# A new order for the attention stretch of a two-block kernel: queries ahead of the convolution's mean, norms behind later work, splits in steps of two tiles

## The chip, the cores and the metric

One core of one Trainium2 chip runs the whole program. The time is the device time of one execution in microseconds (us); the median of three runs counts. A core has five engines with a queue of instructions each: PE (TensorE, matrix products), DVE (VectorE), ACT (ScalarE), POOL (GpSimd) and SP (SyncE, which issues most of the loads). Each works through its queue in program order and waits on counters (semaphores) that other engines raise.

## What is computed

The reference is a chain of two transformer-like blocks on 256 tokens of width 2048, in float32. The change touches the middle of the first block only: the convolution branch, attention, and the beginning of the product with `w_out`.

```python
h = rmsnorm(x, pre_mix_norm)
conv_in, q_lat, kv_lat, k_rope = split(h @ w_in)
a, g = split(conv_in)                       # 1024 channels each
u = causal_depthwise_conv(a * sigmoid(g), conv_w, conv_b)   # 31 taps
u = silu(layernorm(u, conv_ln_g, conv_ln_b))
q = rmsnorm(q_lat, q_norm) @ w_uq           # 8 heads, 128 plain + 64 rotary columns
k_nope, v = rmsnorm(kv_lat, kv_norm) @ w_ukv
attn = causal_attention(q, k, v)            # softmax, 8 heads
mix = concat(rmsnorm(u, conv_out_norm), rmsnorm(attn, attn_out_norm)) @ w_out
x = x + rmsnorm(mix, post_mix_norm)
x = x + rmsnorm(swiglu(rmsnorm(x)), post_ffn_norm)
# second block: pooling mixer, RG-LRU, then 8 heads x 16 experts per token,
# whose rows are gathered from two tables by index
```

## The kernel before

Activations lie transposed in SBUF: a tile is 128 channels by 256 tokens, so 1024 channels are 8 tiles. Weights come through a ring of four 1 MB slots (`raw`); SP issues the load of a unit when the unit four places earlier is no longer used. There are two kinds of units. Plain ones (`w_ukv`, `w_uq`) are used by PE as they are. Those of the wide products (`w_in`, `w_out`, the feed-forward) are split: ACT rounds a piece to a high part (`weights_hi`, into `whi`), DVE subtracts it to get the low part (`weights_lo`, into `wlo`), and the input is split in the same way into `xhi` and `xlo`. A unit is two pieces of 128 output columns over 8 input tiles; for each piece PE issues 8 matmuls of `whi` with 512 columns (both input parts) and 8 of `wlo` with 256 columns (`half_group`). Pieces of `w_out` come in this order: the first half of the input (tiles 0 to 7, the convolution's) for four pieces, then the second half (tiles 8 to 15, attention's) for the same columns. After these eight pieces a loop (`layer`) does the rest.

Nothing schedules the work: the order on each engine is the order in which its block of the program is written, and a wait holds up all that stands behind it in that queue. The names on which the steps below rest:

- `add_taps` (DVE, L1804): the 31 taps of the depthwise convolution, 2 x 31 instructions for each pair of channel tiles, put between other work since the input projection; the remainder runs behind the key rotation.
- the mean (PE, L946): 8 products of a matrix of ones with `conv_a`, waiting for all taps. Its result goes to bank 2; DVE centres the 8 tiles (L1849).
- `head_queries(n, half)` (PE, L922): the queries of head pair n, in two halves of the depth, each from one unit of `w_uq`. ACT copies them out (`queries_out`, L1226). `rotate` (PE, L932) and `rope` (DVE, L1853 to L1857) rotate the 64 rotary columns.
- `pair(n, between)`: `scores` of both heads (PE, L966 and L968), then what `between` holds, then the transposes of the probabilities (L981) and the products with the values (L988, L989). For a head DVE masks and finds the maximum (`head_scores`, L1870 to L1877), ACT takes the exponentials (L1373, L1375), DVE divides (`normalise`, L1884 to L1886), ACT copies the transposes and the outputs.
- A norm goes through three engines: ACT squares the tiles (`norm_squares`, L1238), PE sums them with ones (`norm_total`, L766), DVE takes mean and reciprocal (`norm_inverse`, L1717 and L1720), ACT the root (`norm_root`, L1245), DVE multiplies the tiles (`finish` or `norm_finish`, L1892, L1730). Three norms stand here: `ln` (the layer norm on the centred convolution), `conv` (after Silu, L1395, on ACT) and `attn`.
- `SPLITS` gives at which count of split steps each product's input starts. The input of `w_out` was split in four steps of four tiles.

```python
            pair(0, between_0)
            pair(1, between_1)
            pair(2, lambda: head_queries(3, 1))
            pair(3, lambda: half_group(PIECE0["out1"], 0, PAIRS[0], arriving="out1"))

            half_group(PIECE0["out1"] + 2, 0, PAIRS[1])
            norm_total(NI["attn"], tmp)
            half_group(PIECE0["out1"] + 4, 1, PAIRS[0], arriving="out1")
```

## Time and profile before

| | |
|---|---|
| median of 3 runs | 2808.8 us (2808.61 to 2814.53) |
| the profiled execution | 2809.3 us |
| its span in the profile | 2807.4 us |
| busy PE, DVE, ACT, POOL | 85%, 62%, 28%, 19% of the span |
| mean granted PE clock | 0.975 of full speed |
| the stretch of the change | from 214.3 us (last keys and values) to 347.6 us (loop of `w_out`) |

The profile is one execution. Start times are microseconds from the start of the span. A row of the timeline merges like instructions of one engine: its start, its length, and in brackets the idle time before it with what ended it. PE shows two rows for a float32 product of 128x256, so the 8 products of a total stand as x16. The ends of matmuls are modelled and overlap the next start by some 0.15 us; the time that a block of them takes is therefore read from start to start. A table load (ACT_TABLE_LOAD) is what ACT does when it changes between exponential, Silu and square root. The granted clock is 1.00 at 2.4 GHz and 0.50 at 1.2 GHz.

### The profile page before, as it was taken

The page shows a single profiled execution, that of the slowest core. Times are in us where ns is not written, and L with a number is a line of the kernel's source. Part 1 is how long each engine was busy: PE and PEld are TensorE (multiplying, and loading weights), DVE is VectorE, ACT ScalarE, POOL GpSimd, SP SyncE. Part 2 cuts the span into 40 slices and gives each one's busy share as a digit, 9 for nine tenths or more (in the row PEclk, how much of TensorE's full clock was granted, in tenths as well). Part 3 has the DMA queues.
Part 4 walks back from the last instruction along what each step waited for, and adds up shares of the span by engine and source line. Part 5 has one row for each costly group of instructions (what it writes and reads, how often), then busy time and mean ns, then how long its engine had stood idle before and what let it go on. Part 6 is the DMA issues. An engine that isn't in the chain of part 4 may idle for free.

```text
span 2807.4 us, 29432 instructions
## 1 busy us (share of the span) xinstructions
PE 2379.4 (85%) x10942; PEld 1695.0 (60%) x10942; DVE 1745.5 (62%) x2556; ACT 789.6 (28%) x1156; POOL 520.4 (19%) x594
## 2 busy tenths in 40 slices
PE   8997799999999999899899757777777777777776
PEld 8996688888888888799788622222222232222222
DVE  6985547665666566587657985555655555555444
ACT  5433454443444344545431101001100110111010
POOL 0000010000000000100012343333333333333341
PEclk9999899999999999999999989999999999999999
DMA  6542354556555655554588999999999999999997
GB/s 218 177 129 74 93 177 151 193 181 193 184 190 181 193 180 167 161 165 151 167 256 318 416 421 422 422 422 421 421 422 421 421 421 422 421 421 421 422 422 323
DMA packets 339901, 798.92 MB, mean 285 GB/s; under 512 B 23313, under 2 KB 270699, under 8 KB 273771
## 3 DMA queue, kind: packets, MB, share of 16 engines
q0 software_dynamic: 73728, 536.90, 46.0%
q1 hardware_dynamic: 262971, 257.82, 29.0%
q10 hardware_dynamic: 3120, 3.15, 0.3%
q8 instruction: 47, 0.77, 0.1%
q14 instruction: 35, 0.29, 0.0%
HBM read 795.72 MB, written 2.10 MB: 284 GB/s over the span
## 4 chain that ended last, share of the span: by engine, by line
DMA 38%; PE 12%; DVE 7%; issue 1%; POOL 1%; ACT 1%; DVEq 0%; POOLq 0%; PEldq 0%
DMA row<-in_peer_v,expert 31%; DMA row<-in_peer_u,expert 7%; PE pl L808 4%; DVE row L2269 3%; PE pl L1199 3%; PE pl L815 3%; PE pl L811 1%; PE pl L812 1%; POOL row L719 1%; DVE wlo L1745 1%; DMA raw<-in_w_out 0%; PE pl L1128 0%; DVE x_split L1967 0%; DVE tmp L1958 0%; DVE l_xc L2155 0%
## 5 line engine op out<-in xcount | busy, mean ns | idle before, releaser
L1199 PE MATMUL pl<-row,diag 128*128 128x512 f32 x1856 | 862.1, 608 | 337.7 <-DMA row<-in_peer_v,expert 333.3
L2269 DVE CUSTOM_DVE_ANT_0 row<-row,pg 128x2048 f32<-128x2048 f32 x256 | 582.1, 2287 | 458.0 <-DMA row<-in_peer_u,expert 456.7
L1199 PEld LDWEIGHTS pl<-row,diag 128*128 128x128 f32 x1856 | 338.6, 192 | 861.2 <-issue 467.2
L1745 DVE TENSOR_TENSOR wlo<-raw,whi 128x1024 fp32r<-128x1024 f32 (+1 forms) x436 | 517.3, 1208 | 388.1 <-ACT whi L1226 386.5
L1226 ACT ACTIVATE whi<-raw 128x1024 fp32r<-128x1024 f32 (+1 forms) x436 | 444.1, 1039 | 417.0 <-PE pl L815 400.1
L808 PE MATMUL pl<-x_split,whi 128*128 128x512 f32 x1888 | 479.2, 396 | 23.3 <-DVE x_split L1753 12.0
L808 PEld LDWEIGHTS pl<-x_split,whi 128*128 128x128 f32 x1888 | 342.9, 191 | 87.6 <-issue 13.5
L815 PE MATMUL pl<-x_split,wlo 128*128 128x256 f32 x2656 | 373.5, 284 | 3.8 <-DVE wlo L1745 3.8
L815 PEld LDWEIGHTS pl<-x_split,wlo 128*128 128x128 f32 x2656 | 359.1, 192 | 23.0 <-DVE wlo L1745 4.2
L719 POOL DMA_INDIRECT row<-in_peer_u,expert x256 | 240.9, 941 | 635.5 <-PE pl L1199 504.6
L1647 ACT ACTIVATE diag<-ident,dots 128x128 f32<-128x128 f32 x232 | 90.8, 400 | 889.0 <-PE pl L1199 861.0
L719 POOL DMA_INDIRECT row<-in_peer_v,expert x256 | 252.0, 984 | 168.5 <-issue 65.5
L687 POOL TENSOR_TENSOR sq_sum<-mix 128x512 f32<-128x512 f32 x2 | 2.6, 1292 | 1071.8 <-ACT mix L1508 725.1
L811 PE MATMUL pl<-x_split,whi 128*128 128x256 f32 x768 | 190.2, 285 | 4.6 <-DVE x_split L1753 2.5
L812 PE MATMUL pl<-x_split,whi 128*128 128x256 f32 x768 | 189.1, 284 | 0.0
L808 PE MATMUL pl<-h_split,whi 128*128 128x512 f32 x704 | 179.1, 395 | 4.3 <-DVE h_split L2013 2.2
L811 PEld LDWEIGHTS pl<-x_split,whi 128*128 128x128 f32 x768 | 147.9, 193 | 6.4 <-issue 5.7
L812 PEld LDWEIGHTS pl<-x_split,whi 128*128 128x128 f32 x768 | 148.0, 193 | 0.1
L808 PEld LDWEIGHTS pl<-h_split,whi 128*128 128x128 f32 x704 | 126.7, 190 | 27.1 <-issue 2.6
L1128 PE MATMUL pl<-mix,wq 128*128 128x256 f32 (+1 forms) x576 | 114.0, 360 | 2.3 <-issue 2.3
L1128 PEld LDWEIGHTS pl<-mix,wq 128*128 128x128 f32 x576 | 100.8, 194 | 13.8 <-issue 2.4
L815 PEld LDWEIGHTS pl<-h_split,wlo 128*128 128x128 f32 x704 | 97.7, 191 | 7.7
(331 smaller groups left out, 1528.8 us busy)
## 6 DMA issues: line engine op xcount, KB each, us to landing
raw<-in_w_in SPq DMA_DIRECT2D x50, 1024.0 KB, 5.4
raw<-in_w_gate SPq DMA_DIRECT2D x44, 1024.0 KB, 5.1
raw<-in_w_up SPq DMA_DIRECT2D x44, 1024.0 KB, 5.1
raw<-in_w_out SPq DMA_DIRECT2D x32, 1024.0 KB, 5.4
raw<-in_w_down SPq DMA_DIRECT2D x32, 1024.0 KB, 5.3
wq<-in_peer_wq SPq DMA_DIRECT2D x13, 1024.0 KB, 10.8
raw<-in_w_down SPq DMA_DIRECT2D x16, 768.0 KB, 4.7
raw<-in_w_ukv SPq DMA_DIRECT2D x4, 1024.0 KB, 5.1
```

Source lines behind the costliest of these rows:

```text
L687: nc.gpsimd.tensor_tensor(sq_sum[:], a, b, ALU.add).then_inc(sq_added, 1)
L719: nc.gpsimd.indirect_dma_start(row[b][:], None, A["peer_u_2" if table == "u" else "peer_v_2"][0], bass.IndirectOffsetOnAxis(ap=expert[:, a ...
L808: mm(banks[f], w, xs[:, x].rearrange("p h s -> p (h s)"), start=first_product, stop=(half == 1 and t == k - 1), skip_group_check=True)
L811: mm(banks[f][:, 0:S], w, xs[:, x, 0, :], start=first_product, stop=False, skip_group_check=True)
L812: mm(banks[f][:, 0:S], w, xs[:, x, 1, :], start=False, stop=False, skip_group_check=True)
L815: last = mm(banks[f][:, 0:S], wlo[:, n % 4, t, :], xs[:, half * k + t, 0, :], start=False, stop=(half == 1 and t == k - 1), skip_group_che ...
L1128: last = mm(bank[:, f * S + cols:f * S + cols + width], w[:, t, f, :], mix[:, half * KU + t, cols:cols + width], start=first, stop=(half = ...
L1199: last = mm(pl[q], diag[:, (at - 1) % 4, :], row[b][:, q * 512:(q + 1) * 512], start=(t == 1 and n == 0 and k == 0), stop=last_row, skip_g ...
L1226: return nc.scalar.activation(o, i, ACT.Copy)
L1647: activation(diag[:, (at - 1) % 4, :], ident[:], ACT.Copy, scale=dots[:, c:c + 1]).then_inc(diag_ready, 1)
L1745: V.tensor_tensor(wlo[:, n % 4, 0:k, :], w[:, :, f, :], whi[:, n % 4, 0:k, :].bitcast(F32), ALU.subtract)\
L2269: V.tensor_tensor_reduce(row[b][:], row[b][:], z_tok[:], 1.0, 0.0, ALU.mult, ALU.add, dots[:, at:at + 1])\
```

## The change

The same arithmetic is done, in another order.

1. **PE.** The convolution's mean moves from ahead of the first four `head_queries` and `rotate(0)` to behind them. The total of `ln` moves from ahead of the first scores into `between_0`, behind the queries of the third pair. In `between_1` the total of `conv` moves behind the queries and the rotation. The total of `attn` is cut in two: 4 tiles in `between_2`, 4 between the third and fourth piece of `w_out`.
2. **DVE.** `rope(0)` comes ahead of the centring; the inverse of `ln` comes behind `head_scores`, `normalise` and `rope(1)` of the first pair; the inverse of `conv` comes behind `normalise(3)` and `rope(2)`; the low part of the first `w_out` weights comes ahead of the inverse of `conv`.
3. **ACT.** `queries_out(1)` ahead of the squares of `ln`; `norm_root(ln)` behind the transposes of the first pair; Silu behind the outputs of the first pair; the first `weights_hi` in the second pair instead of the third; the squares of `attn` in two steps of 4 tiles, into `sq_ln` and no longer into `tmp`; the high parts of the pieces 4 to 7 right behind.
4. **Splits of the input of `w_out`** in eight steps of two tiles, on ACT (`out1_hi`), DVE (`out1_lo`) and in PE's waits (`step_of=2`). For the last 8 tiles DVE takes turns: two tiles scaled by the norm, then the low part of the two before.

```diff
-SPLITS = {"in1": 0, "out1": 4, "ffn": 8, "in2": 16, "out2": 24}
+SPLITS = {"in1": 0, "out1": 4, "ffn": 12, "in2": 20, "out2": 28}
...
-            pe.wait_ge(rot_read, 1)
-            pe.wait_ge(conv_step, CONV_K * CT)
-            for t in range(CT):
-                last = mm(pg[2][:, 0:S], ones[:], conv_a[:, t, :], start=(t == 0), stop=(t == CT - 1))
-            last.then_inc(mean_sum, 1)
...
             rotate(0)
-            norm_total(NI["ln"], sq_ln)
+            pe.wait_ge(rot_read, 1)
+            pe.wait_ge(conv_step, CONV_K * CT)
+            for t in range(CT):
+                last = mm(pg[2][:, 0:S], ones[:], conv_a[:, t, :], start=(t == 0), stop=(t == CT - 1))
+            last.then_inc(mean_sum, 1)
...
                 rotate(1)
+                norm_total(NI["ln"], sq_ln)
 
             def between_1():
-                norm_total(NI["conv"], conv_a)
                 head_queries(3, 0)
                 rotate(2)
+                norm_total(NI["conv"], conv_a)
+
+            def between_2():
+                head_queries(3, 1)
+                norm_total(NI["attn"], sq_ln, 0, 4)
+
+            def between_3():
+                half_group(PIECE0["out1"], 0, PAIRS[0], arriving="out1", step_of=2)
...
-            half_group(PIECE0["out1"] + 2, 0, PAIRS[1])
-            norm_total(NI["attn"], tmp)
-            half_group(PIECE0["out1"] + 4, 1, PAIRS[0], arriving="out1")
+            half_group(PIECE0["out1"] + 2, 0, PAIRS[1], between=lambda: norm_total(NI["attn"], sq_ln, 4))
+            half_group(PIECE0["out1"] + 4, 1, PAIRS[0], arriving="out1", step_of=2)
...
+            exponentials(2)
+            exponentials(3)
+            act.wait_ge(conv_silu, CT)
+            norm_squares(NI["conv"], mix, conv_a)
+            weights_hi(u, pc, halves=(0,))
+            prob_out(2)
+            prob_out(3)
+            outputs(2)
+            outputs(3)
+            act.wait_ge(o_ready, 4)
+            activation(sq_ln[:, 0:4, :], mix[:, 8:12, :], ACT.Square).then_inc(norm_sq, 1)
+            norm_root(NI["conv"])
...
+            norm_scale(NI["attn"], HEADS * VH)
+            for t in range(8, DT + 2, 2):
+                if t < DT:
+                    for f in (t, t + 1):
+                        V.scalar_tensor_tensor(mix[:, f, :], mix[:, f, :], col("attn_out_norm", f - 8), rstd[:], ALU.mult, ALU.mult)\
+                            .then_inc(norm_out, 1)
+                if t > 8:
+                    out1_lo(t - 2)
```

PE's queue around the mean, before; `conv_a,ones` is the mean, `q_lat,raw` are the queries, `rotT` is the rotation, `sq_ln,ones` the total of `ln`, the last rows the first scores.

```order
L902 MATMUL pg<-raw,kv_lat 128x256 x8
L946 MATMUL pg<-conv_a,ones 128x256 x8
L922 MATMUL pg<-q_lat,raw 128x256 x3
L922 MATMUL pl<-q_lat,raw 128x256 x6
...
L932 MATMUL pg<-q_pe,rotT 128x256
L766 MATMUL pg<-sq_ln,ones 128x256 x8
L966 MATMUL pl<-k_nope,q_nope 128x128
L968 MATMUL pl<-k_pe,q_pe 128x128
```

And the same place after the change, with the total of `ln` ahead of the transposes of the first pair:

```order
L905 MATMUL pg<-raw,kv_lat 128x256 x8
L925 MATMUL pg<-q_lat,raw 128x256 x3
L925 MATMUL pl<-q_lat,raw 128x256 x6
...
L935 MATMUL pg<-q_pe,rotT 128x256
L956 MATMUL pg<-conv_a,ones 128x256 x8
L968 MATMUL pl<-k_nope,q_nope 128x128
...
L935 MATMUL pg<-q_pe,rotT 128x256
L766 MATMUL pg<-sq_ln,ones 128x256 x8
L983 MATMUL pg<-ident,tmp 128x128 x6
```

The eight matmuls of the mean now stand behind 36 matmuls of queries and one rotation, and the total of `ln` behind the first scores and the third pair's queries.

ACT's queue in the second head pair after the change; L1381 and L1383 are the exponentials, `conv_a<-mix` the squares of `conv`, `whi` the first pieces of `w_out`, `tmp<-pg` the transposed probabilities, `sq_ln<-mix` the first squares of `attn`, L1254 the root of `conv`.

```order
L1381 ACT_TABLE_LOAD [waits pT_done]
L1381 ACTIVATE tmp,small<-tmp,small 128x128 [waits s_max]
L1383 ACTIVATE tmp,small<-tmp,small 128x256
...
L1247 ACTIVATE conv_a<-mix 128x1024 [waits conv_silu]
L1247 ACTIVATE conv_a<-mix 128x1024
L1235 ACTIVATE whi<-raw 128x1024 [waits piece_used,slot_full3]
L1235 ACTIVATE whi<-raw 128x1024 [waits piece_used]
L1235 ACTIVATE tmp<-pg 128x384 [waits o_done,pT_done] x2
L1235 ACTIVATE mix<-pg 128x256 [waits o_done] x2
L1427 ACTIVATE sq_ln<-mix 128x1024 [waits o_ready]
L1254 ACT_TABLE_LOAD [waits norm_out]
L1254 ACTIVATE rstd<-invms 128x256 [waits norm_inv]
```

Before, the squares of `conv` stood between the two outputs of the first pair, the root of `conv` behind the exponentials of the second, and `whi` at the end of the third pair.

## Rows read from the trace of the kernel before

**Rows 1.** Stretches: start:end, us, busy PE PEld DVE ACT POOL, PEclk, DMA share, GB/s
```profile
450.00:1120.00 670.00, 664.95 (x3793) 584.35 (x3792) 409.82 (x427) 282.52 (x307) 0.00 (x0) 1.00 0.58 184
...
1800.00:2807.00 1007.00, 738.35 (x1592) 290.04 (x1592) 553.47 (x786) 105.67 (x239) 370.38 (x382) 0.99 1.00 415
```

**Rows 2.** PE in order of time, 226 to 257 us: start, us, engine, line, what
```profile
226.61 6.43 PE L946 MATMUL pg<-conv_a,ones 128*128 128x256 f32 x16 [12.34 <-DVE conv_a L1804]
...
232.88 1.46 PE L922 MATMUL pg<-q_lat,raw 128*128 128x256 f32 x6
...
248.85 3.62 PE L766 MATMUL pg<-sq_ln,ones 128*128 128x256 f32 x16
...
252.30 0.38 PE L966 MATMUL pl<-k_nope,q_nope 128*128 128x128 f32 x2
...
256.37 1.56 PE L922 MATMUL pg<-q_lat,raw 128*128 128x256 f32 x6
```

**Rows 3.** PE in order of time, from 267 us to the loop of w_out
```profile
267.56 0.55 PE L981 MATMUL pg<-ident,tmp 128*128 128x128 f32 x3 [2.17 <-DVE tmp L1886]
...
282.18 0.82 PE L981 MATMUL pg<-ident,tmp 128*128 128x128 f32 x6
...
284.66 0.39 PE L966 MATMUL pl<-k_nope,q_nope 128*128 128x128 f32 x2
...
305.30 3.75 PE L808 MATMUL pl<-x_split,whi 128*128 128x512 f32 x8 [5.68 <-DVE x_split L1753]
...
334.86 3.53 PE L808 MATMUL pl<-x_split,whi 128*128 128x512 f32 x8 [8.08 <-ACT whi L1226]
...
344.76 2.00 PE L808 MATMUL pl<-x_split,whi 128*128 128x512 f32 x8
...
347.56 2.00 PE L808 MATMUL pl<-x_split,whi 128*128 128x512 f32 x8
```

**Rows 4.** DVE (VectorE) in order of time, 233 to 335 us
```profile
233.53 2.77 DVE L1849 TENSOR_TENSOR conv_a<-conv_a,mean_b 128x256 f32<-128x256 f32 x8
...
253.03 1.75 DVE L1720 RECIPROCAL invms<-meansq 128x256 f32<-128x256 f32 x1
...
257.80 3.25 DVE L1892 SCALAR_TENSOR_TENSOR conv_a<-conv_a,par,rstd 128x256 f32<-128x256 f32 x8
...
266.64 0.16 DVE L1884 RECIPROCAL small<-small 128x2 f32<-128x2 f32 x1
...
299.21 0.55 DVE L1870 SCALAR_TENSOR_TENSOR tmp<-pl,mask 128x384 f32<-128x384 f32 x1
...
300.52 0.56 DVE L1870 SCALAR_TENSOR_TENSOR tmp<-pl,mask 128x384 f32<-128x384 f32 x1
...
332.69 2.43 DVE L1753 TENSOR_TENSOR x_split<-mix,x_split 128x1024 fp32r<-128x1024 f32 x2
```

**Rows 5.** ACT (ScalarE) in order of time, 214 to 305 us
```profile
214.80 1.08 ACT L1226 ACTIVATE v_tok<-pg 128x512 f32<-128x512 f32 x2
...
254.82 0.42 ACT L1245 ACTIVATE rstd<-invms 128x256 f32<-128x256 f32 x1 [5.61 <-DVE invms L1720]
...
255.25 1.28 ACT L1373 ACT_TABLE_LOAD   x1
...
261.08 3.30 ACT L1395 ACTIVATE mix<-conv_a,par 128x256 f32<-128x256 f32 x8 [0.87 <-DVE conv_a L1892]
...
269.93 1.99 ACT L1238 ACTIVATE conv_a<-mix 128x1024 f32<-128x1024 f32 x2
...
302.85 1.99 ACT L1226 ACTIVATE x_split<-mix 128x1024 fp32r<-128x1024 f32 x2
```

**Rows 6.** Two stretches with the granted PE clock, columns as in rows 1
```profile
252.30:299.60 47.30, 44.35 (x201) 32.60 (x199) 29.02 (x74) 26.66 (x59) 0.00 (x0) 1.00 0.29 90
...
305.30:313.41 8.11, 8.11 (x33) 6.98 (x33) 2.41 (x7) 0.00 (x0) 0.00 (x0) 0.67 0.00 0
```

**Rows 7.** DMA issues of the page: size, median us from issue to landing
```profile
raw<-in_w_out SPq DMA_DIRECT2D x32, 1024.0 KB, 5.4
```

More of the change, by code:

```diff
@@ L762, in norm_total @@
                     pe.wait_ge(norm_inv, n)
-                for t in range(tiles):
+                for t in range(t0, t1 or tiles):
                     if t % 4 == 0:
@@ L766, in norm_total @@
                     last = mm(pnorm, ones[:], sq[:, t, :], start=(t == 0), stop=(t == tiles - 1))
-                last.then_inc(norm_sum, 1)
+                if (t1 or tiles) == tiles:
+                    last.then_inc(norm_sum, 1)
             def wide_total(name):
@@ L791, in squares, with half_group @@
                     last.then_inc(norm_sum, 1)
-            def half_group(first, half, banks, xs=x_split, k=KU, i=None, step=0, arriving=None, step_of=4, apart=True):
+            def half_group(first, half, banks, xs=x_split, k=KU, i=None, step=0, arriving=None, step_of=4, apart=True, between=None):
                 for f in range(2):
                     n = first + f
+                    if f and between:
+                        between()
                     pe.wait_ge(w_hi, n + 1 if i is None else i * step + (n + 1))
@@ L1415, in _, with conv_out, out1_hi @@
-            weights_hi(UNIT0["out1"], PIECE0["out1"], halves=(1,))
+            def conv_out(tiles):
+                for c in tiles:
+                    activation(mix[:, c, :], conv_a[:, c, :], ACT.Silu, bias=col("conv_ln_b", c)).then_inc(conv_silu, 1)
+            def out1_hi(t):
+                copy(xhi[:, t:t + 2, :], mix[:, t:t + 2, :]).then_inc(x_hi, 1)
+            u, pc = UNIT0["out1"], PIECE0["out1"]
+            exponentials(0)
+            exponentials(1)
+            queries_out(2)
@@ new lines, in _ @@
+            act.wait_ge(o_ready, 4)
+            activation(sq_ln[:, 0:4, :], mix[:, 8:12, :], ACT.Square).then_inc(norm_sq, 1)
+            norm_root(NI["conv"])
+            exponentials(4)
+            exponentials(5)
+            queries_out(3)
+            prob_out(4)
+            prob_out(5)
+            outputs(4)
+            outputs(5)
+            act.wait_ge(norm_out, tiles_before(NI["conv"] + 1))
+            for t in range(0, 8, 2):
+                out1_hi(t)
+            exponentials(6)
@@ L1416, in _ @@
+            exponentials(7)
+            weights_hi(u, pc, halves=(1,))
+            prob_out(6)
+            prob_out(7)
+            outputs(6)
+            outputs(7)
             act.wait_ge(o_ready, HEADS)
-            norm_squares(NI["attn"], mix[:, 8:16, :], tmp)
+            activation(sq_ln[:, 4:8, :], mix[:, 12:16, :], ACT.Square).then_inc(norm_sq, 1)
+            weights_hi(u + 2, pc + 4, halves=(0,))
             norm_root(NI["attn"])
-            for t in range(8, DT, 4):
-                act.wait_ge(norm_out, tiles_before(NI["attn"]) + t - 4)
-                copy(xhi[:, t:t + 4, :], mix[:, t:t + 4, :]).then_inc(x_hi, 1)
+            for t in range(8, DT, 2):
+                act.wait_ge(norm_out, tiles_before(NI["attn"]) + t - 6)
+                out1_hi(t)
@@ L1424, in gains @@
+            weights_hi(u + 2, pc + 4, halves=(1,))
             def gains(a, name, norm, g, i=None):
@@ L1450, in out @@
                     gains(src, "post_mix_norm", "post", g, i)
-                weights_hi(u + 2, n + 4)
                 out(0)
@@ L1857, in rope @@
                 V.tensor_tensor(q_pe[:, n, :], q_pe[:, n, :], rot[:, n, :], ALU.add).then_inc(roped, 1)
+            add_taps(len(taps))
+            rope(0)
+            dve.wait_ge(mean_sum, 1)
+            link(V.tensor_scalar(mean_b[:], pg[2][:, 0:S], 1.0 / CONV_CH, None, ALU.mult))
+            for c in range(CT):
+                V.tensor_tensor(conv_a[:, c, :], conv_a[:, c, :], mean_b[:], ALU.subtract).then_inc(centred, 1)
             score = tmp[:, 0:4, :].rearrange("p a b -> p (a b)")
@@ L1908, in _ @@
             rope(2)
+            weights_lo(u, pc, halves=(0,))
+            norm_inverse(NI["conv"], CONV_CH)
             dve.wait_ge(conv_silu, CT)
```

74 lines of the change are left out of this document (26 added, 48 removed).

## The prediction

> **What bounds the kernel now.** I began with the busy time by stretch, to see whether time saved in attention reaches the end. In the feed-forward PE works for 665.0 of 670 us, and in the last 1007 us the DMA engines are busy all the time at 415 GB/s, with the gathered rows [rows 1]. Neither stage can make up for a late start or waste an early one: both begin when the stage before hands over, so what the attention stretch loses or wins stands in the total one for one. The question is when the loop of `w_out` starts; now it is at 347.56 [rows 3].
>
> Next, PE in order of time, from the last keys and values on. It waits 12.34 us for the convolution's taps, which keep DVE busy, and then takes the mean, in 6.3 us from start to start although the total of `ln`, equally large, takes 3.45 [rows 2]. Behind that come the queries, which need nothing of the convolution. Later PE waits 5.68 us for the splits of the convolution's tiles and 8.08 us for the weights of piece 4, which stand in ACT's queue behind the norm of attention; after both its 8 wide matmuls take 3.75 and 3.53 us instead of 2.00 [rows 3]. The granted clock tells why: 1.00 (2.4 GHz) through the head pairs, 0.67 over the two pieces behind the wait of 5.68, part of them at 1.2 GHz, so that they take 8.1 us [rows 6]. Between these, a head pair is bound by PE with one short wait (2.17 us) [rows 3].
>
> **The change, part by part.** I lay the new order out in time with the durations of the rows, hand-overs (0.05 to 0.2 us) included.
>
> *Mean behind the queries.* PE can begin when ACT has copied the last values, at 214.80 + 1.08 = 215.9 [rows 5]. Four query halves and a rotation take 248.85 - 232.88 = 16.0 us [rows 2], to 231.9. The taps end at 226.5, when the mean starts today, so they are covered with 5 us to spare; their instructions don't change. The mean at the full clock costs 3.45: 235.3. Today mean, queries and rotation are through at 248.85: 13.5 us earlier. `rope(0)` (1.2 us) falls beside the mean, and the scores can follow at once.
>
> *Total of `ln` behind the first pair's queries.* Scores take 256.37 - 252.30 = 4.1 us [rows 2], the third pair's two halves and rotation 8.2 (half of the 16.0 with one rotation kept), the total 3.45: 251.1. Transposes and values take 284.66 - 282.18 = 2.5 [rows 3]: 253.6. Cover: DVE centres in 2.8 and needs 1.3 for each head's maximum (300.52 - 299.21) [rows 4], to 241.4; ACT squares in 2.0, loads a table in 1.28 and takes two heads' exponentials in 2.0 (302.85 - 300.52 less that 1.3 is one head) [rows 4, 5], to 244.0; dividing takes 0.9 (267.56 - 266.64) [rows 3, 4], to 245.8 for both. So 5 us of slack, and the second scores start 16.6 us earlier than now (267.56 + 2.5 and hand-overs, 270.2).
>
> *The second pair: here the chain leaves PE.* From the end of the total of `ln`: mean and reciprocal 2.2 with the hand-over 0.2, root 0.42, eight tiles 3.25 [rows 4, 5], to 257.5; Silu 3.3, table 1.28, exponentials 2.0, squares 2.0 [rows 5], to 266.0. PE is through with scores, queries and rotation at 262.0 and waits about 3 us, since the total of `conv` can start on the first four squares at 265.1; it ends at 268.5. With transposes and values 271.0, against 284.66 now: 13.7 earlier. The early `weights_hi` costs ACT 1.9 us there but ends by 268, before the transposes are out; its 1 MB has had since PE's use of the third pair's first unit (243.3) and lands in 5.4 [rows 7].
>
> *The third pair.* Output copies, 1.0 of squares, the table, root, eight tiles (3.25), then on DVE two maxima (2.7), an exponential (1.0), a division (0.9), and on PE transpose, rotation, values (2.2): 284.2. Now that point is at 295.4 (305.30 less the wait of 5.68 and scores of 4.1, with the overlap of ends), so the lead is down to 11.2. PE hides the query half and the first half of the `attn` total in this chain.
>
> *Splits by two tiles, weights early.* Four hi copies of half of 1.0 us each [rows 5] and their low parts (half of 1.2 [rows 4]) run from 284.7 to 287.9; scores end at 288.3. So the wait of 5.68 goes, and with it the half clock behind it. Two pieces at 2.8 (347.56 - 344.76) [rows 3], transposes and values 2.5, piece 2, half the total (1.7): 300.9. Then the norm of attention: reciprocal 2.2, root 0.4, two tiles 0.8, hi 0.55, lo 0.65: piece 4 starts at 306.1 and its last split arrives at 309.6, as DVE needs 1.45 per step of two tiles. The rest, 1.4 + 3 x 2.8, ends at **319.5**, against 347.56.
>
> **The sum.** Laid out with the same durations, today's order gives 346.7 (with its slow clock twice, 8.1 - 5.6 = 2.5 and 3.5 - 2.0 = 1.5 us), 0.9 short of the trace; I add 0.8 to the new one: 320.3, or 27.3 us less. Against that stands the clock. The new order keeps two waits of PE, 3 us ahead of the total of `conv` and 2.5 to 3 ahead of piece 4, then 1 us between its steps. Waits of 2.17 cost nothing, those of 5.68 and more cost 1.5 to 2.8 us of slow matmuls each. Between these rows: 0 to 5.6 us; I take 3, since 3 us lies nearer to the small wait but there are two places. That leaves 24.3 us: 2809.3 of the profiled execution becomes 2785.0, and on the median of 2808.8, which is 0.5 lower, **2784.5 us**.
>
> A rule speaks against part of this. The new queue has one table load more (seven in the stretch, six now): root of `ln`, Silu, exponentials again. A row has 1.28 us for one, and the next instruction starts 0.02 behind it [rows 5]. The Trainium skill (ScalarE: Activation LUTs, "What ACT_TABLE_LOAD costs") gives about 2.66 us per switch, drain included. By its figure the sum would be 2788.6, an estimate; I go by the row.
>
> **The rivals.**
>
> *A switch of tables costs more than its row (5%).* The loads ahead of the root of `ln`, of the exponentials behind Silu and of the root of `conv` stand on my chain or at its edge. If ACT loses the row's 1.28 once more at each of three, that is 3.8 us: 2788.3. For it: nothing in the rows; the rule above is the one that says so.
>
> *The norms' chain eats more (10%).* If ACT's order costs a wait that I don't see in the second and third pairs, the lead keeps shrinking as it does from 16.6 to 11.2, and the last part wins nothing: 11.2 us, 2797.6. For it: ACT now holds weights between squares and transposes. Against it: the 8.08 and 5.68 us waits are removed by the order itself.
>
> *The mean's cover fails (3%).* If queries and taps can't run side by side (weights of the second pair not landed, say), 12.3 us of waiting stays and only the last part helps: 13 to 15 us less, 2795.
>
> *No change (3%).* Something later, a weight load for the loop of `w_out`, sets its start. Against it: SP issues by freed slots, and these come free earlier as well.
>
> *Slower: PE falls to 1.2 GHz and stays (3%).* PE now works in small groups with a wait before each: four splits per input half, squares cut in two. If the clock falls there, its work doubles. From 215.9 to 319.5 PE has some 95 us of work at the full clock; once 27 us of it run at half, the gain is gone; were it all, the time would be about 2876, and with half of it 2829. Against it: in the head pairs, with the same small groups, PE was busy 44.35 of 47.30 us and the clock stood at 1.00 [rows 6]. The Trainium skill (TensorE: Matmul & The Clock Gate, "A second HAM failure mode: psum-queue depth-cycling") says that micro-idles between groups of matmuls can make the clock oscillate; this trace doesn't show it for waits as short as these.
>
> **How the numbers follow.** My case has 76%: 2779.5 (no slow clock, a little better hand-overs) to 2791 (two slow starts at 2.8 and 4 us of hand-overs that I missed). It takes in the first rival; the others, 19%, lie outside and fill the two in ten. A measurement of this kernel can tell about 0.2%, 5.6 us. Faster by more: 94%, same 3%, slower 3%.
>
> **What would show it.** The mean (L956) starts near 232 and lasts 3.6 in one block; the second scores start near 254, the third near 271, the fourth near 284, the loop of `w_out` near 320 to 323. PE's wait ahead of the total of `conv` is about 3 us, ended by ACT's squares, and that ahead of piece 4 about 3, ended by the splits. Wrong would be: a wait of PE in the first four query halves, a wait ahead of the first scores, a table load followed by more than 0.1 us of idle ACT with its input there, or a block of slow matmuls longer than 6 us. If the loop starts near 321 and the total falls by much less, the claim on the later stages is what failed.

## The result, and the profile after

The change runs at a median of 2783.86 us (4 runs, 2781.24 to 2784.27) beside 2808.7 us for the kernel before in the same comparison (4 runs, 2807.49 to 2814.53). The ratio is 0.9906, with a 95% interval of 0.9888 to 0.9923, so 22 to 31 us less. The forecast was 2784.5. The profiled execution took 2784.27 us, its span is 25.0 us shorter than that of before.

The page of the kernel after, span and busy time:

```profile
span 2782.4 us, 29442 instructions
...
PE 2373.8 (85%) x10942; PEld 1690.4 (61%) x10942; DVE 1745.8 (63%) x2560; ACT 791.7 (28%) x1161; POOL 521.8 (19%) x594
```

The shares are what they were. Nothing was made cheaper; idle time went. So the place has to be looked for in time. PE of the kernel after, in order of time, with the points that the prediction named:

```profile
215.92 1.53 PE L925 MATMUL pg<-q_lat,raw 128*128 128x256 f32 x6 [1.71 <-issue]
...
231.97 3.62 PE L956 MATMUL pg<-conv_a,ones 128*128 128x256 f32 x16
235.42 0.38 PE L968 MATMUL pl<-k_nope,q_nope 128*128 128x128 f32 x2
...
253.73 0.39 PE L968 MATMUL pl<-k_nope,q_nope 128*128 128x128 f32 x2
...
265.26 5.38 PE L766 MATMUL pg<-conv_a,ones 128*128 128x256 f32 x16 [2.87 <-ACT conv_a L1247]
270.48 0.82 PE L983 MATMUL pg<-ident,tmp 128*128 128x128 f32 x6
...
286.77 0.46 PE L968 MATMUL pl<-k_nope,q_nope 128*128 128x128 f32 x2
...
309.14 0.70 PE L811 MATMUL pl<-x_split,whi 128*128 128x512 f32 x2 [2.56 <-DVE x_split L1929]
310.44 1.22 PE L811 MATMUL pl<-x_split,whi 128*128 128x512 f32 x2 [0.60 <-DVE x_split L1929]
311.84 2.07 PE L811 MATMUL pl<-x_split,whi 128*128 128x512 f32 x4 [0.17 <-DVE x_split L1929]
...
324.47 2.00 PE L811 MATMUL pl<-x_split,whi 128*128 128x512 f32 x8
```

The wait of 12.34 us ahead of the mean [rows 2] is gone, and so are those of 5.68 and 8.08 [rows 3]. Three are new: 1.71 ahead of the queries, which begin when ACT has copied the last values (at 215.9, as laid out), 2.87 ahead of the total of `conv`, 2.56 ahead of piece 4 with gaps of 0.60 and 0.17 behind it. The loop of `w_out`, the last row, starts at 324.47 instead of 347.56 [rows 3].

Behind two of the new waits the clock is down, as the stretches show (start:end, us, busy PE, PEld, DVE, ACT, POOL, granted clock, DMA share, GB/s). The last two rows are the feed-forward and the gathers, to be read beside [rows 1]:

```profile
265.20:270.50 5.30, 5.24 (x17) 4.31 (x18) 3.33 (x5) 2.76 (x3) 0.00 (x0) 0.68 0.29 99
309.10:316.00 6.90, 6.09 (x18) 4.38 (x19) 5.74 (x9) 3.15 (x4) 0.00 (x0) 0.57 0.01 2
...
450.00:1089.00 639.00, 636.75 (x3646) 559.99 (x3645) 388.60 (x403) 267.98 (x289) 0.00 (x0) 1.00 0.58 186
1800.00:2782.00 982.00, 720.32 (x1552) 283.01 (x1552) 538.47 (x758) 103.66 (x234) 361.71 (x372) 0.99 1.00 415
```

What fills the time ahead of the total of `conv` is ACT's queue in the second pair, after the change:

```profile
257.70 3.30 ACT L1399 ACTIVATE mix<-conv_a,par 128x256 f32<-128x256 f32 x8 [1.48 <-DVE conv_a L1925]
261.02 1.28 ACT L1381 ACT_TABLE_LOAD   x1
262.31 0.40 ACT L1381 ACTIVATE tmp<-tmp,small 128x128 f32<-128x128 f32 x1
...
264.08 1.99 ACT L1247 ACTIVATE conv_a<-mix 128x1024 f32<-128x1024 f32 x2
```

Silu ends at 261.0, and a table and two heads' exponentials go ahead of the squares that PE waits for. DVE sets the pace at piece 4, with a low part behind every two scaled tiles:

```profile
308.31 0.68 DVE L1929 TENSOR_TENSOR x_split<-mix,x_split 128x512 fp32r<-128x512 f32 x1
308.91 0.88 DVE L1972 SCALAR_TENSOR_TENSOR mix<-mix,par,rstd 128x256 f32<-128x256 f32 x2
309.70 0.69 DVE L1929 TENSOR_TENSOR x_split<-mix,x_split 128x512 fp32r<-128x512 f32 x1
...
311.09 1.48 DVE L1929 TENSOR_TENSOR x_split<-mix,x_split 128x512 fp32r<-128x512 f32 x2
```

**After the loop starts.** Up to 1092 us of the new trace the low parts of the weights on DVE, which run through all of the loops, stand 23.1 us earlier than their likes of before; then the distance jumps to 24.6. At that place PE has the same wait in both. The kernel before:

```profile
1115.22 2.10 PE L808 MATMUL pl<-h_split,whi 128*128 128x512 f32 x6 [2.03 <-ACT whi L1226]
```

The kernel after:

```profile
1092.15 1.65 PE L811 MATMUL pl<-h_split,whi 128*128 128x512 f32 x6 [2.03 <-ACT whi L1235]
```

The stretch of 5.2 us behind it, before:

```profile
1115.20:1120.40 5.20, 5.18 (x19) 4.39 (x20) 2.58 (x3) 1.48 (x2) 0.00 (x0) 0.67 0.40 101
```

And after:

```profile
1092.10:1097.30 5.20, 5.15 (x28) 4.51 (x29) 2.75 (x3) 2.16 (x3) 0.00 (x0) 1.00 0.39 107
```

Behind the same 2.03 us of idle PE the clock was at 0.67 before and at 1.00 after: 19 matmuls against 28 in equal time. That is 1.5 us that the change got at a place that its edit doesn't touch. The first gather starts 24.6 us earlier (POOL, 1487.37 and 1462.74), the last store 25.1 us (SP's queue, 2802.56 and 2777.46).

The traces of the experiments below show how far such a difference can be trusted. With the two kernels of this case they make fourteen, one trace each. In all of them the wait of 2.03 us (2.02 in some) stands 767.65 to 767.69 us behind the start of the loop, so up to there the gain is handed on whole. Behind it the clock was at 0.67 in seven traces, that of before among them, and at 1.00 in the other seven. From the loop to the end of the span they take 2455.8 to 2461.4 us, though no edit touches these stages; the kernel before has 2459.8, the change 2457.9.

### The profile page after: what moved, and what is told of

It reads as the page before. It is cut to its first block, busy times and chain, and to the rows that moved or that the text cites. A ratio compares the mean times of both kernels' runs of the same rounds, so it can differ in the third digit from the quotient of the medians.

```text
span 2782.4 us, 29442 instructions
## 1 busy us (share of the span) xinstructions
PE 2373.8 (85%) x10942; PEld 1690.4 (61%) x10942; DVE 1745.8 (63%) x2560; ACT 791.7 (28%) x1161; POOL 521.8 (19%) x594
## 4 chain that ended last, share of the span: by engine, by line
DMA 38%; PE 12%; DVE 8%; issue 1%; POOL 1%; ACT 1%; DVEq 0%; POOLq 0%; PEldq 0%
DMA row<-in_peer_v,expert 32%; DMA row<-in_peer_u,expert 6%; PE pl L811 4%; DVE row L2320 3%; PE pl L1208 3%; PE pl L818 3%; PE pl L814 1%; PE pl L815 1%; POOL row L719 1%; DVE wlo L1777 1%; DMA raw<-in_w_out 0%; PE pl L1137 0%; DVE x_split L2018 0%; DVE tmp L2009 0%; DVE l_xc L2206 0%
```

## The experiments

Totals move by 3.0 us among the four runs of the change, and by 8.5 among fourteen runs of the kernel before (2805.62 to 2814.14). So I compare the kernels by marks on PE in the profiled execution: microseconds from the start of PE's last block of values (210.65 before, 210.59 after), which no edit touches. A mark is one execution. "Change" stands for the changed kernel. The last column carries the clock with it: from piece 4 to the loop five kernels with the same steps of DVE and the same wait of 2.56 us take 15.33 (change), 13.98, 14.07, 14.77 and 15.43 us (one more table, conv splits late, squares first, chain shorter). Differences under 1.5 us at the loop can't be told from that.

| kernel | 1st scores | 2nd | 3rd | 4th | piece 0 | piece 4 | loop | time, us (runs) |
|---|---|---|---|---|---|---|---|---|
| before | 41.65 | 59.58 | 74.01 | 84.75 | 94.65 | 124.21 | 136.91 | 2808.7 (4) |
| mean alone | 35.59 | 54.82 | 69.42 | 80.16 | 90.06 | 119.94 | 132.82 | 2802.46 (10) |
| tail as before | 24.83 | 43.15 | 62.37 | 75.09 | 84.73 | 113.96 | 128.01 | 2797.7 (5) |
| conv splits late | 24.83 | 43.15 | 62.38 | 76.18 | 84.26 | 104.65 | 118.72 | 2785.98 (1) |
| weights late | 24.83 | 43.14 | 62.38 | 76.18 | 80.32 | 102.05 | 115.09 | 2782.59 (1) |
| one more table | 24.83 | 43.14 | 64.68 | 78.49 | 82.64 | 100.87 | 114.85 | 2782.47 (1) |
| splits by four | 24.83 | 43.14 | 62.38 | 76.18 | 80.33 | 100.66 | 114.72 | 2783.61 (1) |
| **change** | 24.83 | 43.14 | 62.37 | 76.18 | 80.32 | 98.55 | 113.88 | 2783.86 (4) |
| filled waits | 24.83 | 43.14 | 62.75 | 76.56 | 80.71 | 100.77 | 112.30 | 2784.32 (4) |
| filled to measure | 24.83 | 43.14 | 60.69 | 74.50 | 78.65 | 96.86 | 111.47 | 2782.67 (4) |
| squares first | 24.83 | 43.15 | 60.14 | 73.99 | 78.14 | 96.36 | 111.13 | 2779.87 (4) |
| chain shorter | 24.83 | 43.15 | 57.89 | 70.36 | 74.51 | 92.72 | 108.15 | 2778.89 (4) |
| two pieces abreast | 24.83 | 43.14 | 57.89 | 70.36 | 74.51 | 92.73 | 105.56 | 2775.0 (4) |
| the same, filled | 24.83 | 43.14 | 57.89 | 70.36 | 74.50 | 92.73 | 104.87 | 2775.14 (4) |

The kernel before ran beside each set too, with medians of 2808.6, 2808.51 and 2809.18 us.

### The mean alone

The kernel before, with only the mean moved. So that it can move, `rope(0)` goes ahead of the centring and `queries_out(1)` ahead of the squares of `ln`.

```diff
-            pe.wait_ge(conv_step, CONV_K * CT)
-            for t in range(CT):
-                last = mm(pg[2][:, 0:S], ones[:], conv_a[:, t, :], start=(t == 0), stop=(t == CT - 1))
-            last.then_inc(mean_sum, 1)
...
             rotate(0)
...
+            pe.wait_ge(conv_step, CONV_K * CT)
+            for t in range(CT):
+                last = mm(pg[2][:, 0:S], ones[:], conv_a[:, t, :], start=(t == 0), stop=(t == CT - 1))
+            last.then_inc(mean_sum, 1)
+
             norm_total(NI["ln"], sq_ln)
```

> The kernel before with only the mean moved behind the four query halves and rotate(0) (with rope(0) and queries_out(1) put ahead, which that needs). My theory: the taps' wait of 12.34 us is covered, but the total of ln now has to wait some 4.4 us for the squares of the centred tiles, since it still stands ahead of the first scores. First scores at 243 instead of 252.3, so 9 us less; with a slow PE clock behind that wait 7.5. Loop of w_out near 338.5 to 340. Rival (the mean alone is the whole gain): 13.5 us less or more, loop at 334 or earlier. Rival (cover fails, the queries wait for weights): under 3 us.

The loop came 4.1 us earlier and the time fell to 2802.46 (ratio 0.9976, 0.9966 to 0.9985), where 7.5 to 9 us had been expected. The cover held: the mean started at 231.93 with no wait. But what is behind it is now bare, in PE's time order:

```profile
231.93 3.62 PE L953 MATMUL pg<-conv_a,ones 128*128 128x256 f32 x16
240.05 6.26 PE L766 MATMUL pg<-sq_ln,ones 128*128 128x256 f32 x16 [4.50 <-ACT sq_ln L1238]
...
261.41 0.55 PE L981 MATMUL pg<-ident,tmp 128*128 128x128 f32 x3 [2.17 <-DVE tmp L1887]
```

PE waits 4.50 us for the squares and then takes 6.10 from start to start, 2.65 more than at the full clock. A second slow stretch follows at 262, behind a wait of 2.17 us that stood in the kernel before at the same place [rows 3] and cost nothing there. The two stretches of this kernel:

```profile
240.00:246.20 6.20, 6.15 (x17) 5.02 (x18) 0.00 (x0) 0.85 (x1) 0.00 (x0) 0.58 0.00 0
262.20:265.40 3.20, 3.20 (x12) 2.84 (x13) 0.00 (x0) 1.84 (x4) 0.00 (x0) 0.52 0.22 73
```

and the place of the second in the kernel before:

```profile
268.30:271.60 3.30, 3.25 (x18) 2.49 (x18) 0.00 (x0) 2.78 (x5) 0.00 (x0) 1.00 0.24 79
```

So moving the mean alone gains a third of the 12.34 us that PE waited. The first scores come 6.1 us earlier (at the full clock it would have been 8.7), the second 4.8, and 0.7 more is lost up to the loop. What stood covered behind that wait, ACT's squares of `ln`, comes to light.

### The tail as before

The changed kernel with everything from the splits on as before: steps of four tiles, first weights in the third pair, total of `attn` in one piece, weights of piece 4 last.

```diff
-                norm_total(NI["attn"], sq_ln, 0, 4)
...
-                half_group(PIECE0["out1"], 0, PAIRS[0], arriving="out1", step_of=2)
+                half_group(PIECE0["out1"], 0, PAIRS[0], arriving="out1")
...
+            norm_total(NI["attn"], tmp)
```

> The changed kernel with everything behind the third pair's scores as before: input of w_out split in four steps behind the last exponentials, weights of pieces 4 to 7 late, norm of attention in one go. My theory: the lead of 16.6 us shrinks through the norms' chain to about 12 at the last scores and nothing is won behind them, so the waits of 5.6, 1.5 and 8.1 us stand again. Loop near 336 to 338, 10 to 11.5 us less than before in all. Rival (the tail is worth nothing, its waits were hidden): loop near 325 as in the changed kernel. Rival (front is worth nothing): loop near 347.

The loop came at 128.01: of the 23.0 us of the change 8.9 are from the order of the mean, the totals and what moved with them on ACT and DVE, and 14.1 from the tail. The times say the same, 2797.7 (ratio 0.9962, 0.9948 to 0.9976), 11 and 14 us. So the totals moved along with the mean more than double what the mean gives. All marks up to the third scores are those of the change to 0.01 us, and the lead of 16.8 us at the first scores has shrunk to 9.7 at the fourth. The change's fourth scores come 1.1 us later than these (76.18 and 75.09): that is what the tail's work, put into the third pair, costs there. PE of this kernel shows the two waits of before again:

```profile
294.39 3.75 PE L811 MATMUL pl<-x_split,whi 128*128 128x512 f32 x8 [5.43 <-DVE x_split L1782]
...
323.62 3.78 PE L811 MATMUL pl<-x_split,whi 128*128 128x512 f32 x8 [8.08 <-ACT whi L1235]
```

### Three parts of the tail, each undone by itself

Splits by four tiles instead of two, with DVE scaling all tiles first:

```diff
-                copy(xhi[:, t:t + 2, :], mix[:, t:t + 2, :]).then_inc(x_hi, 1)
+                copy(xhi[:, t:t + 4, :], mix[:, t:t + 4, :]).then_inc(x_hi, 1)
...
+            norm_finish(NI["attn"], mix[:, 8:16, :], "attn_out_norm", mix[:, 8:16, :], HEADS * VH)
+            input_lo("out1", mix, (8, 12))
```

> The changed kernel with the input of w_out split in steps of four tiles instead of two, at the same places. By my layout the first x_lo of attention's tiles comes 2 us later but the last one as early, so the loop starts within 0.3 us of the changed kernel's 324.5 (plus up to 1 us if the longer wait of 4.5 us brings a longer slow clock). Rival (small steps are what wins in the tail): 3 us or more later.

The weights of pieces 4 and 5 behind the splits of attention, on ACT and DVE:

```diff
-            weights_hi(u + 2, pc + 4, halves=(0,))
             norm_root(NI["attn"])
...
-            weights_hi(u + 2, pc + 4, halves=(1,))
+            weights_hi(u + 2, pc + 4)
```

> The changed kernel with the high and low parts of pieces 4 and 5 behind attention's splits, as before. By my layout PE's wait ahead of piece 4 grows from 2.6 to 6.2 us but its steps come without gaps; loop 1.5 us later than 324.5, 2 to 3.5 with a slow clock. Rival (the wait of 8.08 was the weights' and goes with them): 5 us or more later.

The splits of the convolution's tiles behind the last exponentials and, on DVE, behind the last maxima:

```diff
+            exponentials(6)
+            exponentials(7)
             act.wait_ge(norm_out, tiles_before(NI["conv"] + 1))
             for t in range(0, 8, 2):
                 out1_hi(t)
-
-            exponentials(6)
-            exponentials(7)
```

> The changed kernel with the splits of the convolution's tiles behind the last exponentials and maxima, as before, still in steps of two tiles. My theory: here lies the largest part of what the tail wins. PE waits about 3.8 us ahead of piece 0, then 0.2 per step, and DVE comes later to everything behind: loop 4.4 us later by the layout, 6 to 7 with a slow clock, so 118 to 121 us. Rival (the steps of two tiles hide it): under 115.

The loop came 0.84, 1.21 and 4.84 us later. Each of these kernels ran once. PE at piece 4, with splits by four:

```profile
310.27 3.75 PE L811 MATMUL pl<-x_split,whi 128*128 128x512 f32 x8 [4.67 <-DVE x_split L1785]
```

and with the weights late:

```profile
311.63 3.78 PE L811 MATMUL pl<-x_split,whi 128*128 128x512 f32 x8 [6.06 <-ACT whi L1235]
```

Both open the wait by 2 to 3.5 us and yet move the loop by about 1. In the change PE starts earlier but then stops between steps; its last four matmuls begin at 311.84, 101.25 from the mark. By four tiles all eight begin at 100.66, with late weights at 102.05. What sets the end is the last split, so starting on the first is worth little.

How little, an estimate from the rows tells. At the full clock a piece takes 2.79 us. The change's last split ends at 101.98 from the mark, and 1.4 us and three pieces behind it are 111.8. With splits by four, four pieces behind 100.66 are 111.8 too, with late weights 113.2. So the small steps are worth nothing there by themselves and the early weights 1.4 us. The rest is the clock, which took 2.1 us in the change, 2.9 and 1.9 in the two others; as said above, 0.84 and 1.21 can't be told from it.

The early splits of the convolution's tiles are the part with weight. Undone, PE waits ahead of piece 0 again:

```profile
293.77 3.75 PE L811 MATMUL pl<-x_split,whi 128*128 128x512 f32 x8 [3.86 <-DVE x_split L1928]
```

Piece 0 starts 3.94 us later (84.26 for 80.32), and slow matmuls add 2.2 up to piece 4; from there to the loop the clock took 1.3 less than in the change. Together the three differences make 6.9 of the 14.1 us. The rest is in what they do jointly, in the earlier weights of the first pieces and in the total of `attn` cut in two; I did not take these apart.

### Is it the clock? Waits filled with useless matmuls

Extra work is added here: `n` matmuls of the mask by the ones, into a PSUM bank that nobody reads at that time, ahead of the total of `conv` and of piece 4. The two waits on `o_ready` keep them behind the values, whose bank they use. First 12 and 11 of them, then 6 and 5, as one takes 0.43 us (5.18 us from start to start for 12).

```diff
+                pe.wait_ge(o_ready, 2)
+                fill(12)
                 norm_total(NI["conv"], conv_a)
...
+            pe.wait_ge(o_ready, HEADS)
+            fill(11)
             half_group(PIECE0["out1"] + 4, 1, PAIRS[0], arriving="out1", step_of=2)
```

> The changed kernel with matmuls of no use in PE's two longest waits (12 ahead of the total of conv, 11 ahead of piece 4; they write a bank that nothing reads then). From the start of PE's last block of values to the loop of w_out it is 113.9 us in the changed kernel, 136.9 before. My theory: the total of conv takes 5.2 us instead of 3.45 and pieces 4 and 5 take 9.75 instead of some 7.8 only because the clock falls in these waits; filled, both go: 1.8 + 1.9 less, so 110.2 us, and 3 to 4 us in all. Rival (the total waits for its second squares, pieces 4 and 5 for their splits and weights): no change, 113.9. Rival (the clock falls by something else than the wait): partly, 112 or more.

> The changed kernel with 6 useless matmuls ahead of the total of conv and 5 ahead of piece 4, which is what fits into the waits of 2.87 and 2.56 us (one takes 0.43; the run before had 12 and 11, which pushed both points 2.2 us back and ate what the clock gave). My theory: total of conv in 3.45 us at its old start, 54.7 us behind PE's last block of values, pieces 4 and 5 without slow matmuls: 109.8 to 110.5 us to the loop instead of 113.9. Rival (only long filling holds the clock): 112 or more.

With 12 and 11, PE:

```profile
261.24 5.34 PE L1007 MATMUL pg<-mask,ones 128*128 128x256 f32 x24
266.42 3.62 PE L766 MATMUL pg<-conv_a,ones 128*128 128x256 f32 x16
...
305.81 4.91 PE L1007 MATMUL pg<-mask,ones 128*128 128x256 f32 x22
310.37 2.38 PE L811 MATMUL pl<-x_split,whi 128*128 128x512 f32 x8
```

and its clock there:

```profile
266.40:270.00 3.60, 3.60 (x19) 3.12 (x18) 2.02 (x2) 0.57 (x1) 0.00 (x0) 1.00 0.02 5
310.30:317.20 6.90, 6.90 (x38) 5.78 (x38) 3.98 (x6) 3.13 (x4) 0.00 (x0) 1.00 0.17 40
```

The filling was 2.2 us too long each time (marks 56.8 and 100.77 for 54.67 and 98.55), and still the loop starts 1.6 us earlier than in the change, because nothing behind it runs slowly. Its 112.30 is far from the 110.2 that I had expected and lies where I had put the rival of another cause, at 112 or more. But at piece 4 this kernel starts late, when all splits are there, so it doesn't part a held clock from late input.

The shorter filling does, for the first wait. With 6 and 5 the total of `conv` starts when it does in the change and the third scores come 1.7 us earlier, which is the price of that wait alone. Unfilled, the same wait (2.87 or 2.88 us) is followed by the same slow total (a row of 5.38 us) in all five kernels of the table that have this order: change, tail as before, conv splits late, weights late, splits by four. So it is PE's idling that brings the clock down there. The loop starts 2.4 us earlier, at 111.47 where 109.8 to 110.5 had been expected. The filling ahead of piece 4 did not show: from there to the loop it takes 14.61 us, within the 13.98 to 15.43 of the kernels without it. PE of that kernel at the total of `conv` and at piece 4:

```profile
264.33 3.69 PE L766 MATMUL pg<-conv_a,ones 128*128 128x256 f32 x16 [0.28 <-ACT conv_a L1256]
...
309.21 2.04 PE L811 MATMUL pl<-x_split,whi 128*128 128x512 f32 x4 [0.66 <-DVE x_split L1938]
```

The long wait was filled there, to 0.40 us, but the steps of DVE leave gaps of 0.6, and behind these the clock fell to 0.54 for 3.7 us:

```profile
309.20:312.90 3.70, 3.69 (x13) 3.18 (x14) 3.05 (x3) 1.91 (x3) 0.00 (x0) 0.54 0.00 0
```

The rule of the Trainium skill that I had set against the change (TensorE: Matmul & The Clock Gate, "A second HAM failure mode: psum-queue depth-cycling") says that micro-idles between groups of matmuls make the clock swing between its levels. This trace agrees in part: behind gaps of 0.4 to 0.66 us it fell to 0.54 once, and did not swing.

In the total the filling is not to be seen: 2784.32 and 2782.67, ratios 0.9911 and 0.9907 with the change's 0.9906. In the trace of the longer filling the stages behind the start of the loop took 2461.4 us, 3.5 more than the change's, which is more than it had won.

### One more change of tables

A square root of a 128x1 tile between Silu and the exponentials, an addition that nothing uses, makes ACT load one table more on the chain to the total of `conv`.

```diff
             conv_out(range(CT))
+            activation(small[:, 63:64], ones[:, 0:1], ACT.Sqrt)
```

> The changed kernel with one square root of 128x1 between Silu and the exponentials of the third head, which makes ACT change tables once more on the chain. By the row of 1.28 us the chain grows by 1.28 and about 0.2 for the instruction: 115.4 us from PE's last block of values to the loop. Rival (a change costs 2.66 us, as the Trainium skill's page ScalarE: Activation LUTs states under What ACT_TABLE_LOAD costs): 116.7.

ACT of this kernel:

```profile
259.89 1.28 ACT L1416 ACT_TABLE_LOAD   x1
261.18 0.20 ACT L1416 ACTIVATE small<-ones 128x1 f32<-128x1 f32 x1
261.39 1.28 ACT L1381 ACT_TABLE_LOAD   x1
```

and PE:

```profile
265.64 6.19 PE L766 MATMUL pg<-conv_a,ones 128*128 128x256 f32 x16 [4.38 <-ACT conv_a L1247]
```

The total of `conv` starts 56.18 from the mark instead of 54.67, so 1.51 us later: the load's 1.28 and the root's 0.20. A switch costs its row here. The change's own trace says the same at its other loads: where its input was there, the next instruction starts within 0.02 us of the load's end. The 2.66 us of the Trainium skill (ScalarE: Activation LUTs, "What ACT_TABLE_LOAD costs") would have made 2.9, an estimate with the root's 0.20. The rival that a table costs more than its row has fallen. What comes on top is PE's clock: the wait is longer by 1.5, and the total takes 0.8 more. At the loop only 0.97 of the 2.3 are left, since from piece 4 to the loop it takes 13.98 us for the change's 15.33, with the same waits.

### What the chain leaves on the table

Three steps, each on top of the one before. First the squares of `conv` go ahead of the exponentials of the second pair:

```diff
-            exponentials(2)
-            exponentials(3)
             act.wait_ge(conv_silu, CT)
             norm_squares(NI["conv"], mix, conv_a)
+            exponentials(2)
+            exponentials(3)
```

> The changed kernel with the squares of conv ahead of the exponentials of the third and fourth head on ACT. My theory: the chain from Silu to the total of conv is what PE waits 2.87 us for; it gets 3.3 us shorter (table and two exponentials), PE's wait and the slow clock behind it go, but then the transposes wait about 1 us for the probabilities. 1.1 us less by the layout and 1.8 by the clock: 111 us to the loop, 2.5 to 3.5 us less in all. Rival (DVE's maxima or ACT set the pace of this pair anyway): 113.5 or more.

Then Silu takes each tile as DVE has scaled it, and the third pair's maxima and divisions go ahead of the scaling of `conv`:

```diff
-            act.wait_ge(norm_out, tiles_before(NI["ln"] + 1))
-            conv_out(range(CT))
+            for c in range(CT):
+                act.wait_ge(norm_out, tiles_before(NI["ln"]) + c + 1)
+                conv_out([c])
...
-            finish(NI["conv"], mix, "conv_out_norm")
...
             normalise(5)
+            dve.wait_ge(conv_silu, CT)
+            finish(NI["conv"], mix, "conv_out_norm")
```

> The run with conv's squares first (111.1 us to the loop), and Silu waiting tile by tile for DVE instead of for all eight, and the maxima and divisions of the third pair ahead of the eight multiplications of conv on DVE. My theory: Silu starts 1.5 us earlier, the third pair's scores follow by 1.4, and the fourth's by another 0.9, as the eight multiplications (3.25 us) leave PE's chain: 2.3 us less, 108.8 to the loop. Rival (PE and not these chains sets the pace by now): 110.5 or more.

Then the high passes of pieces 4 and 5 take turns tile by tile, so that a split that has arrived gives PE two matmuls instead of one, and the weights' low passes of both follow:

```diff
-            half_group(PIECE0["out1"] + 4, 1, PAIRS[0], arriving="out1", step_of=2)
...
+            for t in range(KU):
+                if t % 2 == 0:
+                    pe.wait_ge(x_lo, SPLITS["out1"] + (KU + t) // 2 + 1)
+                for f in range(2):
+                    mm(pl[f], whi[:, (n + f) % 4, t, :], x_split[:, KU + t].rearrange("p h s -> p (h s)"), start=False,
+                       stop=(t == KU - 1), skip_group_check=True)
...
```

> The run before, and PE takes pieces 4 and 5 abreast, step by step of two tiles. My theory: the gaps of 0.6 us between the steps take piece 5's matmuls, which saves half of its 1.84 us and more, 1.4 us: 107.4 to the loop; the slow clock may take up to 1 us of it. Rival (the last split's arrival plus PE's remainder is the same in both orders): no change.

And five useless matmuls ahead of that:

```diff
+            pe.wait_ge(o_ready, HEADS)
+            fill(5)
```

> The run before, with 5 useless matmuls in the wait ahead of pieces 4 and 5. My theory: no slow clock there, 1 to 2 us less: 105.5 to 106.5 us to the loop, 7.5 to 8.5 less than the changed kernel's 113.9; in the total, whose later stages shift by up to 2 us with the clock, 2774 to 2779. Rival (the clock isn't held by such matmuls in between, or the total does not follow): over 2780.

The loop starts at 111.13, 108.15, 105.56 and 104.87. PE in the first of them:

```profile
261.26 3.69 PE L766 MATMUL pg<-conv_a,ones 128*128 128x256 f32 x16
...
267.55 0.70 PE L990 MATMUL pg<-tmp,v_tok 128*128 128x256 f32 x2 [0.80 <-ACT tmp L1235]
```

The wait of 2.87 is gone at the total of `conv`; 0.38, 0.33 and 0.80 remain ahead of the transposes and the values, and behind them the clock is at 0.67:

```profile
267.50:272.60 5.10, 5.05 (x17) 3.67 (x17) 4.20 (x4) 3.31 (x5) 0.00 (x0) 0.67 0.00 0
```

In the third, PE at pieces 4 and 5:

```profile
302.32 5.50 PE L1035 MATMUL pl<-x_split,whi 128*128 128x512 f32 x16 [2.56 <-DVE x_split L1943]
307.66 2.07 PE L1040 MATMUL pl<-x_split,wlo 128*128 128x256 f32 x16
```

The 2.56 us stays, but no idle time shows inside the 16 matmuls that follow. The loop comes 2.6 us earlier. An estimate from the rows gives the order 1.4 of these: behind the last split (ended at 305.75) the rest at the full clock is 8.4 us instead of 9.8. The other 1.2 are a clock that took less. The stretch from the start of piece 4, without and with the five useless matmuls:

```profile
302.30:309.20 6.90, 6.88 (x29) 5.71 (x30) 5.72 (x9) 3.16 (x4) 0.00 (x0) 0.75 0.00 0
303.50:310.40 6.90, 6.56 (x34) 5.14 (x35) 5.70 (x9) 3.31 (x5) 0.00 (x0) 1.00 0.00 1
```

The third kernel takes 2775.0 us (2772.9 to 2775.8; ratio 0.9881, 0.9865 to 0.9898). It beats both kernels of this case: 34.2 us less than before in the same set, and 8.9 less than the median of the change, which ran in another set. The totals of the neighbours in this row of steps (2778.89 and 2775.0, four runs each) have intervals that overlap. Filling the last wait as well brings the loop 0.7 us forward with the clock at 1.00, as the second row shows, and leaves the time where it is, 2775.14.

## Why the prediction was right, and where it was off

**The cover of the mean: as laid out.** 231.97 for 231.9, first scores at 235.42, 16.8 us earlier, with no wait of PE ahead of them. The second scores were to start at 253.6 and did at 253.73.

**The second pair: the chain as read, the clock on top.** The total of `conv` was to start at 265.1 after about 3 us; it did at 265.26 after 2.87, ended by ACT's squares. The third scores were laid out at 271.0 and came at 272.96: the total takes 5.22 us instead of 3.45. That the kernels with this wait filled or reordered win 1.7 and 2.2 us at the third scores shows that it was the wait.

**The third pair.** The lead was to fall to 11.2 us and fell to 8.6 (fourth scores at 286.77, before at 295.40). 1.8 of the difference of 2.6 is that slow clock, some 0.8 are hand-overs and what the third pair's added work costs beyond its place in the layout. This is the mechanism of my second rival, the norms' chain that eats the lead, going a little further than I had it; it did not eat the gain of the tail, which was the rival's claim.

**The tail.** The waits of 5.68 and 8.08 went; piece 4 starts after a wait of 2.56 (about 3 was said), ended by the splits, in steps of 1.39 us (1.45 was said). From the last split, which DVE ends at 312.57, to the loop at 324.47 it takes 11.9 us where 1.4 and three times 2.8 were laid out, 9.8: 2.1 for the clock. What was loose is the account of why the tail gains. The text gave the small steps a place of their own. Undone by themselves they move the loop by 0.84 us, which can't be told from the clock; the early splits of the convolution's tiles move it by 4.8, of which 3.9 stand at piece 0 already.

**The sum.** The loop was laid out at 319.5, with 0.8 for hand-overs and 3 for the clock: 323.3. It starts at 324.47. The clock took 3.9 (1.8 and 2.1) and the hand-overs 1.1. So the stretch gave 23.1 us where 24.3 were said. The 3 for the clock was a choice between bounds of 0 and 5.6, and the other traces say how wide it was: ahead of the total of `conv` 1.8 each time, at piece 4 between 0.8 and 2.2 behind the same wait of 2.56.

**One for one: as said to the feed-forward, and behind it luck.** Up to the wait at 767.7 us behind the loop's start the gain is handed on whole. Then 1.9 us come on top: 1.5 are the clock that fell behind a wait of 2.03 us at 1115 before and did not after, the rest comes in the gathers. Both lie inside the 5.6 us by which the later stages differ among the fourteen traces. So that the total came within 0.7 us of the forecast is luck: the stretch gave 1.2 us less than said, and this made up for it. With the later stages as the kernel before had them the time would have been near 2786, inside the range.

**The rivals.** A table that costs more than its row: fallen by the experiment. The mean's cover failing, and no change: not seen. PE at 1.2 GHz for long: no, the slow stretches last 5 to 7 us. But the text had named a block of slow matmuls longer than 6 us as a sign that it was wrong, and that at piece 4 is one: 6.9 us at 0.57, with the gaps of DVE's steps in it. It cost 2.1 us and not the gain, so the sign was drawn too tight for what it was to show.

## What to carry to other kernels

Where an engine waits for a late result, look in its own queue for work that doesn't need it, then ask what stood behind the wait: here the mean alone gave 4 us, the mean with the totals behind it 9. When the first engine's waits are covered, the path leaves it for the chain of the next norm through ACT and DVE, and there the order of two neighbours in a queue is worth more than it looks: here the squares ahead of the exponentials gave 2.2 us at the next scores and 2.8 at the loop. A finer step helps only as far as the first piece is what the consumer waits for; where it is the last, give the consumer twice the work for each piece that arrives, so that less is left behind the last one (here 1.4 us less).

## What the runs showed of the hardware that I had not expected

- One and the same wait of PE is followed by a slow clock in one kernel and not in the next: 2.17 us (0.52 and 1.00) and 2.03 us (0.67 and 1.00). The first is worth 1.3 us, the second 1.5, so small differences in a total say nothing by themselves. Behind the wait of 2.03 the clock was down in seven of fourteen traces. The marks inside the trace told kernels apart that the totals did not, down to some 1.5 us; below that they carry the same chance.
- A wait of 2.87 us, which I had placed near the harmless one of 2.17, cost 1.8 us in each of five traces. One of 2.56, with short gaps behind it, cost 0.8 to 2.2 us in five (estimates, against the layout at the full clock). Gaps of 0.3 to 0.8 us in a row were enough too, with the long wait ahead of them filled or gone (0.54 and 0.67), though in the change's third pair two of 0.29 and 0.61 were not (1.00).
- Useless matmuls in a wait kept the clock at 1.00, at 0.43 us for each of 128x256 in float32, but an overshoot of 2 us ate most of what they brought, and where short gaps followed (0.60 and 0.66) the clock fell all the same.
